# A long convolution by matrix transforms: even frequencies folded a second time, odd ones paired, 36 table blocks a round in place of 48

## The chip, the cores and the metric

The kernel runs on one core of a Trainium2 chip. The metric is the device time of one execution in microseconds, all of the network below included. An execution goes through two transformer-like blocks; the change touches one part of the first of them, the "Hyena" long convolution, and what stands just ahead of it and just behind it.

## The reference, cut to what matters

Two gated convolutions over the whole sequence (L = 1024 tokens, 512 channels). Each multiplies the spectrum of the signal by that of a two-sided filter of 2L taps. The filter is computed by a small network and weighted with a decay.

```python
def _hyena_filter_spectrum(L, w1, b1, fr1, w2, b2, fr2, w3):
    ...
    filt = filt * jnp.exp(-t * jnp.abs(deltas))[:, None, None, :]
    fwd = filt[:, :, 0]
    bwd = jnp.flip(filt[1:, :, 1], axis=0)
    two_sided = jnp.concatenate([fwd, zeros, bwd], axis=0)
    return jnp.fft.rfft(two_sided, axis=0)

def _hyena(hy, spec, skip):
    z, g1, g2 = u[..., :D_HYENA], u[..., D_HYENA:2 * D_HYENA], u[..., 2 * D_HYENA:]
    for o, gate in enumerate((g1, g2)):
        conv = jnp.fft.irfft(jnp.fft.rfft(z, n=2 * L, axis=1) * spec[:, o], n=2 * L, axis=1)[:, :L]
        z = gate * (conv + z * skip[o].astype(jnp.float32))
    return z
```

Ahead of it `hy = _short_conv_centred(proj[..., :HY_COLS], ...)` makes the signal and the gates (a matmul and three taps per channel), and behind it stands `_group_rms_norm(_hyena(hy, spec, hy_skip[l]), hy_norm_g[l], HYENA_GROUPS)`.

## The kernel before

Every fp32 operand is split in a rounded high part and a low part (`Split`), and a product of two of them is three matmuls (`mm3`, lines 193 to 195). The high part is made by ScalarE, the low part by VectorE or GpSimd, which subtract.

**The projection (`phase_conv_proj`, 230 to 428 us of the span).** Twelve tiles of 128 channels. For tile n TensorE does 96 matmuls in two halves; between the halves it makes filter taps (line 714), which need two psum banks that VectorE clears in `weigh` (lines 732, 733). Then ScalarE copies the tile out of psum (lines 892, 893), VectorE adds the two neighbouring taps (lines 932, 935), and TensorE turns the tile by eight transposes (line 848) one tile later. VectorE's program in a tile is: the two neighbour taps, `fold` of one filter tile (line 763; in the first tile of each filter four copies of one row, line 768), `weigh`. Tokens lie in the order 0 to 512, then 1023 down to 513, so that cosines and sines need one half of the sequence.

**The convolution (`phase_convolve`, 428 to 728 us).** Two rounds, one per gate. A round has three stages of 16 units; a unit is one table block of 4 x 128 x 128 numbers and, on TensorE, 12 matmuls of 128x512, apart from the `exact` rows and columns (lines 1011, 1012: two matmuls each).
- Filter stage (`filter_pe`): the filter's spectrum. It needs the four blocks of the folded filter (1 MB each, loaded, rounded by ScalarE in `fold_high`, line 1181, lowered by VectorE in `fold_low`, line 1252). ScalarE copies the result (lines 1210, 1211), which frees the banks (`act_free`).
- Signal stage (`signal_pe`): the signal's spectrum, two units for each of eight frequency tiles j. VectorE multiplies with the filter's spectrum (lines 1285 to 1288, `dve_done`), GpSimd adds the cross terms (lines 1241, 1242, `pool_done`), ScalarE rounds (lines 1188, 1189, `w_hi`), VectorE lowers (line 1258, `y_lo`).
- Inverse stage (lines 1147 to 1167): back to tokens. Tile j is read out by ScalarE and VectorE (lines 1227, 1298, 1299), multiplied with the gate (line 1308) and, in the second round, squared and summed (lines 1315, 1316), while TensorE goes on with tile j + 1.

The tables go through a ring of four buffers: SyncE loads block u when TensorE has finished unit u - 4 (line 983), ScalarE rounds it (`high`, line 988), GpSimd lowers it (`low`, line 993), and TensorE waits for that (`ft_lo`). What sets the order is the program of each engine as it is written: an engine that waits holds all that stands behind it. `until(u)` on ScalarE says how far it runs ahead with `high` before it waits for something else:

```python
            def until(u):
                while ahead[0] < min(u + 3, 2 * ROUND):
                    tables.high(act, ahead[0])
                    ahead[0] += 1
```

and GpSimd runs four table blocks ahead:

```python
                for j in range(TT):
                    for u in (B + UNITS + 2 * j + 4, B + UNITS + 2 * j + 5):
                        tables.low(pool, u)
                    pool.wait_ge(R.sem("dve_done"), R.at("dve_done", j + 1))
```

## Time and profile before

| | us |
|---|---|
| median of 3 runs (lowest, highest) | 3569.22 (3565.95, 3570.24) |
| the profiled execution | 3566.57 |
| its span, first to last instruction | 3564.8 |
| projection, convolution, group norm in it | 230 to 428, 428 to 728, 728 to 742 |
| TensorE, VectorE, ScalarE, GpSimd busy (share of the span) | 3332.7 (93%), 1758.4 (49%), 1112.2 (31%), 560.6 (16%) |
| mean granted TensorE clock | 0.971 |

The times of the rows are microseconds from the start of the span. Successive matmuls overlap in the records, so what one costs is the distance between two starts, not its duration.

### The profile page before, as it was taken

The numbers are of one execution on the slowest core, as the hardware profiler recorded it, in microseconds if no ns is written. First come the engines' busy times: TensorE is split into PE (matmuls) and PEld (weight loads), VectorE is DVE, ScalarE is ACT, GpSimd is POOL, SyncE is SP. The second block draws the span as 40 slices with busy tenths as digits, with TensorE's granted clock in tenths as the row PEclk, the third lists the DMA queues.
The fourth block names the chain that finished last, engine by engine and source line by source line (L and its number), as shares of the span: only waits on it lengthen the run. The fifth ranks groups of instructions, "written<-read, shape, count | busy, mean of one in ns | idle before, by whom it ended". The sixth has DMA issues, their size and how long they took to land. (4 is left out here: it accounts for less than half of the span.)

```text
span 3564.8 us, 40485 instructions
## 1 busy us (share of the span) xinstructions
PE 3332.7 (93%) x15544; PEld 2663.5 (75%) x15544; DVE 1758.4 (49%) x2739; ACT 1112.2 (31%) x2015; POOL 560.6 (16%) x378
## 2 busy tenths in 40 slices
PE   7999899976898899999999998988999899999998
PEld 5777688865786678888888776775567688888886
DVE  4415655565422446555544539789654332332434
ACT  4323344354322222111111433136674221211112
POOL 0002466722000001000001200000263200010010
PEclk9999999987999999999999999999999999999999
DMA  3232324412121113333321301123333121111111
GB/s 115 87 104 70 130 88 136 142 61 92 54 71 59 42 59 95 100 102 105 104 83 62 105 18 42 48 57 90 76 73 113 30 71 48 47 47 47 51 43 59
DMA packets 223644, 269.80 MB, mean 76 GB/s; under 512 B 17277, under 2 KB 150294, under 8 KB 221062
## 3 DMA queue, kind: packets, MB, share of 16 engines
q1 hardware_dynamic: 223496, 267.78, 24.4%
q8 instruction: 98, 1.61, 0.2%
q14 instruction: 50, 0.41, 0.0%
HBM read 219.16 MB, written 29.18 MB: 70 GB/s over the span
## 5 line engine op out<-in xcount | busy, mean ns | idle before, releaser
L193 PE MATMUL psum<-rounded,rounded 128*128 128x512 f32 (+2 forms) x3936 | 1537.7, 391 | 64.6 <-DVE rounded L222 51.6
L194 PE MATMUL psum<-rounded,rounded 128*128 128x512 f32 (+2 forms) x3936 | 1528.7, 388 | 0.0
L195 PE MATMUL psum<-rounded,rounded 128*128 128x512 f32 (+2 forms) x3936 | 1528.2, 388 | 0.0
L193 PEld LDWEIGHTS psum<-rounded,rounded 128*128 128x128 f32 x3936 | 746.6, 190 | 239.1 <-DVE rounded L222 56.8
L195 PEld LDWEIGHTS psum<-rounded,rounded 128*128 128x128 f32 x3936 | 746.1, 190 | 151.8
L194 PEld LDWEIGHTS psum<-rounded,rounded 128*128 128x128 f32 x3936 | 747.2, 190 | 148.9 <-issue 0.2
L3002 DVE TENSOR_TENSOR plain<-psum,plain 128x512 f32<-128x512 f32 x432 | 288.6, 688 | 110.4 <-PE psum L195 108.8
L3013 DVE TENSOR_TENSOR plain<-psum,plain 128x512 f32<-128x512 f32 x44 | 30.4, 692 | 425.1 <-ACT plain L2917 425.1
L3579 POOL TENSOR_TENSOR plain<-plain,plain 128x128 f32<-128x128 f32 (+3 forms) x64 | 97.3, 1530 | 563.4 <-ACT plain L3680 506.4
L3376 DVE TENSOR_SCALAR_CACHE_REDUCE plain<-plain,plain 128x384 bf16<-128x384 f32 (+2 forms) x204 | 181.8, 942 | 1.4
L2994 DVE TENSOR_TENSOR rounded<-plain,rounded 128x512 fp32r<-128x512 f32 x108 | 96.9, 897 | 166.0 <-ACT rounded L2906 165.9
L2917 ACT ACTIVATE plain<-psum 128x512 f32<-128x512 f32 x44 | 26.3, 598 | 454.6 <-PE psum L195 454.6
L2965 POOL TENSOR_TENSOR plain<-plain 128x512 f32<-128x512 f32 x64 | 67.0, 1047 | 597.2 <-ACT plain L2919 597.2
L993 POOL TENSOR_TENSOR rounded<-plain,rounded 128x512 fp32r<-128x512 f32 x96 | 143.6, 1505 | 101.2 <-ACT rounded L988 101.2
L2977 POOL TENSOR_TENSOR plain<-plain,plain 128x1024 f32<-128x1024 f32 x22 | 52.6, 2395 | 658.0 <-DMA plain<-in_w_down_dram 658.0
L2919 ACT ACTIVATE plain<-psum 128x512 f32<-128x512 f32 x64 | 38.3, 599 | 374.4 <-PE psum L195 374.4
L2941 ACT ACTIVATE rounded<-plain 128x1024 fp32r<-128x1024 f32 x54 | 57.0, 1056 | 278.4 <-DMA plain<-in_ff_w_dram 157.2
L3601 DVE CUSTOM_DVE_ANT_0 plain<-psum,plain 128x128 f32<-128x128 f32 (+7 forms) x128 | 96.2, 754 | 96.1 <-PE psum L3184 35.8
L3507 PE MATMUL psum<-plain,plain 128*128 128x128 f32 x576 | 86.9, 278 | 28.2 <-ACT plain L3664 26.8
L3653 ACT ACTIVATE plain<-plain,plain 128x128 f32<-128x128 f32 (+7 forms) x128 | 99.0, 773 | 37.5 <-DVE plain L3601 36.4
L988 ACT ACTIVATE rounded<-plain 128x512 fp32r<-128x512 f32 x96 | 60.5, 632 | 147.3 <-DMA plain<-in_c_fwd_dram 96.6
L2376 ACT ACTIVATE plain<-psum 128x1024 f32<-128x1024 f32 (+1 forms) x33 | 28.8, 872 | 237.1 <-PE psum L195 237.1
(326 smaller groups left out, 3457.5 us busy)
## 6 DMA issues: line engine op xcount, KB each, us to landing
plain<-in_ff_w_dram SPq DMA_DIRECT2D x64, 512.0 KB, 5.4
plain<-in_w_ada_dram SPq DMA_DIRECT2D x96, 256.0 KB, 3.5
plain<-in_w_gu_dram SPq DMA_DIRECT2D x44, 512.0 KB, 5.0
plain<-in_w_in_dram SPq DMA_DIRECT2D x36, 512.0 KB, 4.0
rounded<-rounded SPq DMA_DIRECT2D x72, 256.0 KB, 3.4
plain<-in_c_fwd_dram SPq DMA_DIRECT2D x64, 256.0 KB, 2.6
plain<-in_w_down_dram SPq DMA_DIRECT2D x22, 512.0 KB, 3.7
fold<-plain SPq DMA_DIRECT2D x8, 1024.0 KB, 4.8
```

Source lines behind the costliest of these rows:

```text
L193: nc.tensor.matmul(out, wh, xh, start=first, stop=False)
L194: nc.tensor.matmul(out, wh, xl, start=False, stop=False)
L195: return nc.tensor.matmul(out, wl, xh, start=False, stop=last)
L993: self.core.nc.gpsimd.tensor_tensor(w.lo, w.raw, w.hi_raw, ALU.subtract).then_inc(S["ft_lo"].sem, 1)
L2965: nc.gpsimd.tensor_tensor(full[half], first[half], first[half], ALU.mult).then_inc(S["square_done"].sem, 1)
L2994: nc.vector.tensor_tensor(ft[b].lo[:, f, cols], full[half], ft[b].hi_raw[:, f, cols], ALU.subtract).then_inc(S["ft_lo"].sem, 1)
L3002: nc.vector.tensor_tensor(hv, ps[:, 4 + t % 4, :], hv, ALU.add).then_inc(S["dve_free"].sem, 1)
L3376: self.after(nc.vector.tensor_scalar(self.flags[c % 2][:, 0:w], sel_tile(self.core, i), self.bound[:, c:c + 1], None, op, ALU.add, accum_o ...
L3507: last = nc.tensor.transpose(ps[:, 4 + j // 4, (j % 4) * P:(j % 4 + 1) * P], probs[n % 3][:, j * P:(j + 1) * P], core.ident)
L3579: nc.gpsimd.tensor_tensor(masked(n)[:, 0:w], slanted[h % 2][:, L - w:L], sel_tile(core, i), ALU.add).then_inc(S["pool_done"].sem, 1)
L3601: nc.vector.tensor_tensor_reduce(out=probs[n % 3][:, 0:w], in0=pair(n, w), in1=b, scale=-SCALE, scalar=3.0e38, op0=ALU.add, op1=ALU.min, a ...
L3653: nc.scalar.activation(probs[n % 3][:, 0:w], probs[n % 3][:, 0:w], ACT.Exp, scale=-1.0, bias=least[:, one], accum_out=total[:, one]).then_ ...
```

## The change

- Tokens lie in a new order (even and odd ones apart, `TOKENS`, `COLUMNS`), so that signal and inverse fold twice for even frequencies and in pairs for odd ones. The four tokens on the fold's edges are kept in four columns beside the tile (`t[:, L:L + 4]`).
- A round has 16 units in the filter stage as before, 12 in the signal stage and 8 in the inverse stage. In matmuls: filter 206 for 210, signal 166 for 210, inverse 114 for 210, which is 486 for 630 in a round.
- In the projection ScalarE has one more instruction per tile, VectorE three more small taps and a copy of four columns; `fold` copies a row in the second tile of each filter too.
- VectorE mends two pairs of rows of the loaded filter (`fix_folds`) before any `fold_low` but the first of round 1, and folds the signal in two steps of 1024 elements (`fold_signal`).
- GpSimd runs three table blocks ahead, and no block of the inverse stage is lowered ahead of the last cross terms. In the signal stage ScalarE runs fewer blocks ahead, and waits for the pairing (`paired`).
- The inverse stage's results stay in psum and in `kept_sums` until all of a parity are there; adding, gating and squaring come after the last of them.
- The group norm no longer mirrors (no `reverse`), and writes to strided columns.

```diff
 
                 ins.then_inc(S["fold_chain"].sem, 1)
-                dve.wait_ge(S["fold_chain"].sem, S["fold_chain"].at(4 * o + q + 1))
-                ins = nc.vector.tensor_copy(out[0:1, :], (a if q % 2 else b)[0:1, :])
+                dve.wait_ge(S["fold_chain"].sem, S["fold_chain"].at(8 * o + 4 * j + q + 1))
+                row = ((0, 0, 3, 2), (0, 2, 1, 3))[j][q]
+                ins = nc.vector.tensor_copy(out[0:1, :], self.both[0:1, row, :])
         ins.then_inc(S["pair_folded"].sem, 1)
 
     def close(self):
...
+                        last = nc.tensor.transpose(ps[:, 4 + t // 4, (t % 4) * P:(t % 4 + 1) * P], tmp[m % 2][:, TOKENS[t]], core.ident)
                     last.then_inc(S["tr_done"].sem, 1)
...
                 w1, bias = core.colsA[:, CW_HY + 12 + n:CW_HY + 13 + n], core.colsA[:, CB_HY + n:CB_HY + n + 1]
-                nc.scalar.activation(tmp[n % 2][:, 0:513], pr[:, 0:513], ACT.Identity, scale=w1, bias=bias)
-                nc.scalar.activation(tmp[n % 2][:, 513:L], pr[:, L - 1:512:-1], ACT.Identity, scale=w1, bias=bias).then_inc(S["act_done"].sem, 1)
+                t, pr2 = tmp[n % 2], quarters(pr)
+                nc.scalar.activation(quarters(t)[:, :, 1:256], pr2[:, :, 1:256], ACT.Identity, scale=w1, bias=bias)
+                nc.scalar.activation(quarters(t)[:, :, 257:512], pr2[:, :, 511:256:-1], ACT.Identity, scale=w1, bias=bias)
...
+                chain(last)
+                nc.vector.tensor_copy(t[:, 0:L].rearrange("p (b a c) -> p a b c", a=2, b=2)[:, :, :, 0], t[:, L:L + 4].rearrange("p (a b) -> p a b", a=2)).then_inc(S["dve_done"].sem, 1)
                 if 1 <= f <= NF:
                     filters.fold(dve, f - 1)
                 if 0 <= f < NF:
                     filters.weigh(dve, f, 0)
     for n in ("mm_done", "dve_done", "act_free", "tr_done", "act_done", "w_hi", "w_lo"):
         S[n].close(n_tiles)
-    S["dve_chain"].close(n_tiles)
+    S["dve_chain"].close(2 * n_tiles)
...
+            tables.products(pe, one, B + n, zfold, cos, True, j >= 2)
+            if j < 2:
+                exact(nc, one, mats[:, ALT_ROW, :], quarter, 0, last=True, rows=1)
+            ins = tables.products(pe, two, B + n, zfold, sin, True, j != 0, block=2)
+            if j == 0:
+                exact(nc, two, mats[:, ONE_COL, :], zfold, 0)
+                exact(nc, two, mats[:, NEG_COL, :], zfold, 1)
+                ins = exact(nc, two, mats[:, ONE_COL, :], quarter, 0, last=True, rows=1)
+            ins.then_inc(done, 1)
+        else:
+            u = B + 2 * n - 4
+            tables.products(pe, one, u, zfold, range(4, 8), True, True).then_inc(done, 1)
+            tables.products(pe, two, u + 1, zfold, range(0, 4), True, False)
+            mm3(nc, two, eighth[0:1, 0, :], eighth[0:1, 1, :], quarter.hi[0:1, 0, :], quarter.lo[0:1, 0, :], False, True).then_inc(done, 1)
...
+            n = 2 * p + part
+            one, two = ps[:, 2 * n, :], ps[:, 2 * n + 1, :]
+            src = Y_S if part else Y_R
+            pe.wait_ge(R.sem("dve_done"), R.at("dve_done", 5 + n))
+            pe.wait_ge(R.sem("y_lo"), R.at("y_lo", 4))
+            tables.products(pe, one, B + n, y, (src, src + 1), True, False)
+            ins = tables.products(pe, two, B + n, y, (src + 2, src + 3), True, False, block=2)
+            if part == 0:
+                ins = exact(nc, one, mats[:, NEG_ROW if p else ONE_ROW, :], y, Y_S, rows=1)
+            elif p == 0:
+                exact(nc, one, mats[:, ONE_COL, :], y, Y_R)
+                exact(nc, one, mats[:, ONE_COL, :], y, Y_R + 1)
+                ins = exact(nc, one, mats[:, ONE_COL, :], y, Y_S, rows=1)
...
+                        nc.scalar.activation(quarter.hi[0:1, 0, :], quarter.raw[0:1, 0, :], ACT.Copy).then_inc(R.sem("z_hi"), 1)
+                for n in range(4):
+                    until(B + signal_done(n))
+                    act.wait_ge(R.sem("pool_done"), R.at("pool_done", n + 1))
+                    nc.scalar.activation(y.hi[:, n::TT, :], y.raw[:, n::TT, :], ACT.Copy).then_inc(R.sem("w_hi"), 1)
+                for b in range(2):
+                    until(B + signal_done(5 + 2 * b))
+                    act.wait_ge(R.sem("paired"), R.at("paired", b + 1))
+                    nc.scalar.activation(y.hi[:, 4 + b:TT:2, :], y.raw[:, 4 + b:TT:2, :], ACT.Copy)
+                    nc.scalar.activation(y.hi[:, TT + 4 + b::2, :], y.raw[:, TT + 4 + b::2, :], ACT.Copy).then_inc(R.sem("w_hi"), 1)
+                until(B + INVERSE_AT + 4)
+                if R.o == 0:
...
-                        tables.low(pool, u)
-                    pool.wait_ge(R.sem("dve_done"), R.at("dve_done", j + 1))
+                low = B + SIGNAL_AT + 3
+                for n, j in enumerate(SIGNAL_ORDER):
+                    while low < min(B + signal_done(n) + 3, B + INVERSE_AT):
+                        tables.low(pool, low)
+                        low += 1
+                    pool.wait_ge(R.sem("dve_done"), R.at("dve_done", n + 1))
                     nc.gpsimd.tensor_tensor(yr[:, j, :], yr[:, j, :], cross[:, j, :], ALU.subtract)
-                    nc.gpsimd.tensor_tensor(ys[:, j, :], ys[:, j, :], cross[:, 8 + j, :], ALU.add).then_inc(R.sem("pool_done"), 1)
-                for u in range(B + 2 * UNITS + 4, B + ROUND):
...
+                if R.o == 0:
+                    fix_folds(R)
+                    for n in range(4):
+                        fold_low(R, n)
+                fold_signal(R)
                 if R.o == 1:
-                    dve.wait_ge(rounds[0].sem("tile_gated"), rounds[0].at("tile_gated", 4))
...
+                def pair(b):
+
+                    dve.wait_ge(R.sem("pool_done"), R.at("pool_done", 6 + 2 * b))
+                    one, two = y.raw[:, 4 + b::TT, :], y.raw[:, 6 + b::TT, :]
+                    chain(nc.vector.tensor_tensor(one, one, two, ALU.add))
+                    nc.vector.scalar_tensor_tensor(out=two, in0=two, scalar=-2.0, in1=one, op0=ALU.mult, op1=ALU.add).then_inc(R.sem("paired"), 1)
+
...
+                            last = nc.vector.tensor_tensor(terms[:, p, 3, :], other, own, ALU.subtract)
+                    last.then_inc(R.sem("dve_free"), 1)
+                if R.o == 0:
+                    fix_folds(rounds[1])
+                    fold_low(rounds[1], 1)
...
+                dve.wait_ge(R.sem("dve_free"), R.at("dve_free", 2))
+                for p in range(2):
+                    near, far = hy[:, 2 * p:2 * p + 2, 0:DH], hy[:, 4 + 2 * p:6 + 2 * p, 0:DH]
+                    nc.vector.tensor_tensor(near, terms[:, p, 0:2, :], terms[:, p, 2:4, :], ALU.add)
+                    chain(nc.vector.tensor_tensor(far, terms[:, p, 0:2, :], terms[:, p, 2:4, :], ALU.subtract))
...
+                        chain(nc.vector.tensor_tensor(hy[0:1, 4, 0:DH], u, rows[1], ALU.subtract))
+                    for n, (made, t) in enumerate(((near, 2 * p), (far, 4 + 2 * p))):
+                        nc.vector.tensor_tensor(made, made, gates[:, t:t + 2, :], ALU.mult).then_inc(R.sem("tile_gated"), 1)
+                        if R.o == 1:
+                            dve.wait_ge(R.sem("tile_gated"), R.at("tile_gated", 2 * p + n + 1))
+                            chain(nc.vector.tensor_tensor(squares, made, made, ALU.mult))
```

What stands on the engines in a row, at three places. In these listings `rounded_512` are the table blocks, `rounded_8192` and `plain_8192` the product y or the filter's blocks, `plain_12288` the signal and the gates.

GpSimd, before, from the cross terms of the seventh frequency tile of a signal stage on:

```order
L1241 TENSOR_TENSOR plain_8192_57<-plain_8192_57,plain_8192_58 128x512 [waits dve_done]
L1242 TENSOR_TENSOR plain_8192_57<-plain_8192_57,plain_8192_58 128x512
L993 TENSOR_TENSOR rounded_512_1502<-plain_512_1503,rounded_512_1501 128x512 [waits ft_hi]
L993 TENSOR_TENSOR rounded_512_1506<-plain_512_1507,rounded_512_1505 128x512 [waits ft_hi]
L1241 TENSOR_TENSOR plain_8192_57<-plain_8192_57,plain_8192_58 128x512 [waits dve_done]
L1242 TENSOR_TENSOR plain_8192_57<-plain_8192_57,plain_8192_58 128x512
L993 TENSOR_TENSOR rounded_512_1494<-plain_512_1495,rounded_512_1493 128x512 [waits ft_hi]
L993 TENSOR_TENSOR rounded_512_1498<-plain_512_1499,rounded_512_1497 128x512 [waits ft_hi]
```

and GpSimd now, from the same tile on:

```order
L1364 TENSOR_TENSOR plain_8192_57<-plain_8192_57,plain_8192_58 128x512 [waits dve_done]
L1365 TENSOR_TENSOR plain_8192_57<-plain_8192_57,plain_8192_58 128x512
L1364 TENSOR_TENSOR plain_8192_57<-plain_8192_57,plain_8192_58 128x512 [waits dve_done]
L1365 TENSOR_TENSOR plain_8192_57<-plain_8192_57,plain_8192_58 128x512
L1071 TENSOR_TENSOR rounded_512_1494<-plain_512_1495,rounded_512_1493 128x512 [waits ft_hi]
L1071 TENSOR_TENSOR rounded_512_1498<-plain_512_1499,rounded_512_1497 128x512 [waits ft_hi]
L1071 TENSOR_TENSOR rounded_512_1502<-plain_512_1503,rounded_512_1501 128x512 [waits ft_hi]
```

Before, four blocks of the inverse stage are lowered ahead of the last cross terms (lines 1241, 1242) or with them; now the first block of the inverse stage comes behind the last cross terms (lines 1364, 1365).

ScalarE, before, in a signal stage, from the first rounding of y on:

```order
L1188 ACTIVATE rounded_8192_55<-plain_8192_57 128x512 [waits pool_done]
L1189 ACTIVATE rounded_8192_55<-plain_8192_57 128x512
L988 ACTIVATE rounded_512_1493<-plain_512_1495 128x512 [waits table0]
L988 ACTIVATE rounded_512_1497<-plain_512_1499 128x512 [waits table1]
L1188 ACTIVATE rounded_8192_55<-plain_8192_57 128x512 [waits pool_done]
L1189 ACTIVATE rounded_8192_55<-plain_8192_57 128x512
L988 ACTIVATE rounded_512_1501<-plain_512_1503 128x512 [waits table2]
L988 ACTIVATE rounded_512_1505<-plain_512_1507 128x512 [waits table3]
L1188 ACTIVATE rounded_8192_55<-plain_8192_57 128x512 [waits pool_done]
L1189 ACTIVATE rounded_8192_55<-plain_8192_57 128x512
```

and ScalarE now:

```order
L1333 ACTIVATE rounded_8192_55<-plain_8192_57 128x2x512 [waits pool_done]
L1066 ACTIVATE rounded_512_1493<-plain_512_1495 128x512 [waits table0]
L1333 ACTIVATE rounded_8192_55<-plain_8192_57 128x2x512 [waits pool_done]
L1066 ACTIVATE rounded_512_1497<-plain_512_1499 128x512 [waits table1]
L1333 ACTIVATE rounded_8192_55<-plain_8192_57 128x2x512 [waits pool_done]
L1066 ACTIVATE rounded_512_1501<-plain_512_1503 128x512 [waits table2]
L1333 ACTIVATE rounded_8192_55<-plain_8192_57 128x2x512 [waits pool_done]
L1066 ACTIVATE rounded_512_1505<-plain_512_1507 128x512 [waits table3]
L1066 ACTIVATE rounded_512_1493<-plain_512_1495 128x512 [waits table0]
L1066 ACTIVATE rounded_512_1497<-plain_512_1499 128x512 [waits table1]
```

Before there are two table blocks between two roundings of y; now one, for the first four, and then four blocks.

VectorE, before, from the end of the first round's inverse stage to the signal's fold of the second:

```order
L1308 TENSOR_TENSOR plain_12288_1492<-plain_2048_2891,plain_12288_1492 128x512 [waits dve_free]
L1308 TENSOR_TENSOR plain_12288_1492<-plain_2048_2891,plain_12288_1492 128x512
L1252 TENSOR_TENSOR rounded_8192_56<-plain_8192_54,rounded_8192_55 128x2048 [waits fold_hi] x2
L1268 TENSOR_TENSOR plain_4096_2886<-plain_12288_1492 128x512 [waits tile_gated]
L1271 COPY plain_4096_2886<-plain_12288_1492 1x512 [waits dve_chain]
L1268 TENSOR_TENSOR plain_4096_2886<-plain_12288_1492 128x512 x4
L1271 COPY plain_4096_2886<-plain_12288_1492 1x512 [waits dve_chain]
L1268 TENSOR_TENSOR plain_4096_2886<-plain_12288_1492 128x512 x3
```

and VectorE now, from the repaired rows of the second round's filter to its last `fold_low` (of the gating and of `fold_signal`, 20 instructions, those left out by the two pieces are of the same kinds):

```order
L1388 SCALAR_TENSOR_TENSOR plain_8192_54<-plain_8192_54 1x512 [waits dve_chain]
L1388 SCALAR_TENSOR_TENSOR plain_8192_54<-plain_8192_54 1x512
L1375 TENSOR_TENSOR rounded_8192_56<-plain_8192_54,rounded_8192_55 128x2048 [waits fold_hi]
L1479 TENSOR_TENSOR plain_12288_1492<-plain_4096_2986 128x2x512 [waits dve_free]
L1480 TENSOR_TENSOR plain_12288_1492<-plain_4096_2986 128x2x512
L1483 TENSOR_TENSOR plain_12288_1492<-plain_2048_2985,plain_512_2984 1x512 [waits dve_chain]
L1484 TENSOR_TENSOR plain_12288_1492<-plain_2048_2985,plain_512_2984 1x512
```

```order
L1401 TENSOR_TENSOR plain_4096_2976<-plain_4096_2977 128x1024 [waits dve_chain]
L1402 TENSOR_TENSOR plain_4096_2976<-plain_4096_2977 128x1024
L1401 TENSOR_TENSOR plain_4096_2976<-plain_4096_2977 128x1024
L1402 TENSOR_TENSOR plain_4096_2976<-plain_4096_2977 128x1024
L1405 TENSOR_TENSOR plain_4096_2976<-plain_12288_1492 1x512 [waits dve_chain]
L1406 COPY plain_4096_2976<-plain_12288_1492 1x512
L1408 TENSOR_TENSOR plain_512_2980<-plain_12288_1492 1x512
L1375 TENSOR_TENSOR rounded_8192_56<-plain_8192_54,rounded_8192_55 128x2048 [waits fold_hi] x2
```

Before, the two last `fold_low` (line 1252, x2) stand ahead of the signal's fold; now they stand behind all of the gating (lines 1479 to 1488) and of the fold (lines 1395 to 1408).

## Rows read from the trace of the kernel before

**Rows 1.** The page, part 1: busy us, share of the span, instructions.
```profile
PE 3332.7 (93%) x15544; PEld 2663.5 (75%) x15544; DVE 1758.4 (49%) x2739; ACT 1112.2 (31%) x2015; POOL 560.6 (16%) x378
```

**Rows 2.** Waits of TensorE, 433.5 to 722: total, times, longest.
```profile
PE psum L193 <- DVE rounded L1252: 6.8, 1, 6.8
```

**Rows 3.** Stretches: length, then busy us and count of each engine, clock.
```profile
core 0: us, PE busy (x) PEld busy (x) DVE busy (x) ACT busy (x) POOL busy (x), PEclk, DMA share, GB/s
433.00:438.00 5.00, 4.54 (x11) 3.57 (x12) 4.45 (x3) 4.07 (x3) 4.83 (x2) 0.50 1.00 371
500.00:560.00 60.00, 60.00 (x265) 49.48 (x264) 37.62 (x41) 21.35 (x37) 49.87 (x35) 1.00 0.48 158
```

**Rows 4.** Groups of 433.5 to 722: count, busy us, mean ns, idle before.
```profile
L193 PE MATMUL psum<-rounded,rounded 128*128 128x512 f32 x384 | 150.6, 392 | 6.8 <-DVE rounded L1252 6.8
L1012 PE MATMUL psum<-rounded,rounded 128*128 128x512 f32 x54 | 21.0, 389 | 0.0
L1241 POOL TENSOR_TENSOR plain<-plain,plain 128x512 f32<-128x512 f32 x16 | 27.0, 1684 | 0.0
L988 ACT ACTIVATE rounded<-plain 128x512 fp32r<-128x512 f32 x93 | 58.8, 632 | 146.4 <-DMA plain<-in_c_fwd_dram 96.6 <-DMA plain<-in_c_inv_dram 49.8
```

**Rows 5.** Timeline of VectorE and ScalarE at the first round's start: start, duration.
```profile
431.11 2.29 DVE L1252 TENSOR_TENSOR rounded<-plain,rounded 128x2048 fp32r<-128x2048 f32 x1 [4.02 <-ACT rounded L1181]
436.76 1.91 ACT L1181 ACTIVATE rounded<-plain 128x2048 fp32r<-128x2048 f32 x1 [0.88 <-DMA plain<-fold]
```

**Rows 6.** Timeline of TensorE at the first round's start.
```profile
433.46 0.80 PE L193 MATMUL psum<-rounded,rounded 128*128 128x512 f32 x1 [6.75 <-DVE rounded L1252]
```

**Rows 7.** Timeline of the projection, VectorE and TensorE.
```profile
311.16 0.42 DVE L768 COPY plain<-plain 1x512 f32<-1x512 f32 x1
314.93 1.55 PE L714 MATMUL psum<-plain,plain 64*128 64x512 f32 x3 [1.36 <-DVE plain L733]
395.52 0.68 DVE L733 TENSOR_TENSOR plain<-psum,plain 128x512 f32<-128x512 f32 x1
396.63 1.98 PE L714 MATMUL psum<-plain,plain 64*128 64x512 f32 x4
404.12 1.03 PE L848 MATMUL psum<-plain,plain 128*128 128x128 f32 x8
```

**Rows 8.** Timeline of VectorE: an instruction of 4 columns, in another stage.
```profile
766.34 0.16 DVE L2081 SCALAR_TENSOR_TENSOR plain<-psum,plain 128x4 f32<-128x4 f32 x1 [1.92 <-PE psum L1926]
```

**Rows 9.** Timeline of the signal stage, GpSimd, VectorE, ScalarE.
```profile
496.38 1.29 POOL L1241 TENSOR_TENSOR plain<-plain,plain 128x512 f32<-128x512 f32 x1
498.88 1.29 POOL L993 TENSOR_TENSOR rounded<-plain,rounded 128x512 fp32r<-128x512 f32 x1
499.61 0.68 DVE L1288 TENSOR_TENSOR plain<-psum,plain 128x512 f32<-128x512 f32 x1
502.17 2.55 DVE L1258 TENSOR_TENSOR rounded<-plain,rounded 128x512 fp32r<-128x512 f32 x2 [1.88 <-ACT rounded L1189]
502.43 1.74 POOL L1241 TENSOR_TENSOR plain<-plain,plain 128x512 f32<-128x512 f32 x1
504.64 0.68 DVE L1285 TENSOR_TENSOR plain<-psum,plain 128x512 f32<-128x512 f32 x1
```

**Rows 10.** Timeline of ScalarE: one pass over 1024 elements.
```profile
389.61 1.02 ACT L863 ACTIVATE plain<-psum 128x1024 f32<-128x1024 f32 x1
```

**Rows 11.** Timeline of VectorE at the second round's start.
```profile
581.91 5.58 DVE L1252 TENSOR_TENSOR rounded<-plain,rounded 128x2048 fp32r<-128x2048 f32 x2
589.23 1.40 DVE L1271 COPY plain<-plain 1x512 f32<-1x512 f32 x1
```

**Rows 12.** Timeline of the convolution's end, TensorE, ScalarE and VectorE.
```profile
719.11 0.60 ACT L1227 ACTIVATE plain<-psum 128x512 f32<-128x512 f32 x1 [4.46 <-PE psum L195]
721.40 0.39 PE L195 MATMUL psum<-rounded,rounded 128*128 128x512 f32 x1
725.73 1.23 DVE L1315 TENSOR_TENSOR plain<-plain 128x1024 f32<-128x1024 f32 x1
726.99 1.22 DVE L1316 TENSOR_REDUCE plain<-plain 128x16 f32<-128x1024 f32 x1
730.39 0.55 DVE L1355 RECIPROCAL plain<-plain 128x64 f32<-128x64 f32 x1 [2.18 <-ACT plain L1375]
```

540 lines of the change are left out of this document (309 added, 231 removed).

## The prediction

> **What bounds the kernel now.** I read the page's busy line first: TensorE is busy for 3332.7 us of the span, 93%, and no other engine reaches half [rows 1]. So the convolution's time is the number of its matmuls times their pitch, as long as TensorE waits for nothing there. The waits of that stretch say so: one wait, 6.8 us, at its start [rows 2]; the grouped lines give the same 6.8 for all 384 matmuls of a line and 0.0 for the exact rows [rows 4]. A stretch of 60 us in the middle gives the pitch: 60.00 busy, 265 matmuls, clock 1.00, so 0.2265 us each [rows 3]. It also warns: GpSimd is busy for 49.87 of these 60 us. It is the engine with the least room, and every table block goes through it. Behind the one wait 11 matmuls take 4.54 us at a granted clock of 0.50 [rows 3], 0.41 each: a long wait of TensorE costs some 2 us more than itself. Both together: 1260 x 0.2265 = 285.4, plus 12 x 0.19, is 287.7; the stretch took 721.8 - 433.5 = 288.3 [rows 6, 12].
>
> **A. Matmuls removed.** 630 - 486 is 144 in a round, 288 in both. 288 x 0.2265 = **-65.2 us**, if TensorE stays as busy as now. Sixty of the new matmuls contract over one row; I count them like the others, and no row shows one. The Trainium skill ("TensorE: Matmul & The Clock Gate", Why this matters for your kernels) says a matmul with small K takes the time of a full one; that agrees with the count. Were they free instead, 60 x 0.2265 = 13.6 us more would go; that is in the lower end.
>
> **B. Projection.** A tile's chain is psum full, ScalarE's copy, the neighbour taps, `fold`, `weigh`, TensorE's line 714. In an ordinary tile `weigh` ends at 395.52 + 0.68 = 396.20 and TensorE starts at 396.63: 0.43 us of room; in a filter's first tile it waits 1.36 already [rows 7]. The chain gets one more small instruction on ScalarE and four of four columns or fewer on VectorE. An instruction of 4 columns took 0.16 [rows 8]; with their order among themselves I take 0.75 a tile. Two first tiles +0.75 each; two second tiles also get four row copies at 0.42 [rows 7], +1.8 + 0.75 - 0.43 = 2.1 each; three others and the last +0.3 to 0.75; clock +1. **+8.5**, bounds 3 and 13. The transposes read tokens with a stride; eight take 1.03 [rows 7]. I cost that at nothing; if each took twice as long, the 96 would add 12.4.
>
> **C. First round's start.** `fold_low` (2.29, from 431.11) led straight to the first matmul at 433.46 [rows 5, 6]. Now `fix_folds` stands ahead of it on VectorE and waits for the fourth filter block, which lands just ahead of ScalarE's 436.76 [rows 5]. Then four row operations at about 0.6 (between the copy's 0.42 and the 1.40 of one of them beside GpSimd [rows 7, 11]) and `fold_low`: 436.76 + 2.4 + 2.3 = 441.5, which is **+8.0**, bounds 6 and 10.
>
> **D. Signal stage, twice.** Before, ScalarE has two table blocks between two roundings of y; now one, for the first four. So `high` of unit 20 waits for the GpSimd sums of the first tile, and so on for units 21 to 23, while GpSimd's next `low` waits for that `high`. One turn is: two cross terms, 2 x 1.29 alone or 2 x 1.74 beside VectorE's lowering (1.69 on average); rounding of 1024 elements 1.02; `high` 0.63; `low` 1.29 [rows 4, 9, 10]. That is 5.5 to 6.4 us, for a unit that TensorE eats in 12 x 0.2265 = 2.7 (3.4 with its exact ones). Four turns cost about 4 x 2.8, less the two blocks in store, some 6 to 8. Then unit 27 stands behind the first pairing (products 0.68 each, sums 2 x 1.3, pair 2 x 1.3, rounding 2.0, `high`, `low`), some 6 more. With 2 of clock the stage lasts about 54 against 166 x 0.2265 = 37.6: **+16.5** each, **+33**, bounds 10 and 21 each.
>
> What the rows show of the two engines: the same cross term takes 1.29 us while VectorE reads psum and 1.74 while it subtracts two SBUF operands [rows 9]. The Trainium skill ("GPSIMD Engine Reference", 1. Specifications) says that GpSimd shares its SBUF interfaces with VectorE and collides with instructions of two SBUF inputs; the trace agrees. The pairing is such an instruction, 1024 elements long. By the rule the sums beside it take 3.5 a pair, without it 2.6: 0.9 a turn, within my bounds.
>
> **E. Inverse stage's start, twice.** The first inverse block is lowered behind the last cross terms; before, four were ahead. TensorE ends the signal stage; then VectorE's products 2.6 (four at 0.68), the sums 2.6 to 3.5, `low` 1.3: 6.5 to 7.4 us, of which I take 7.4 since the pairing runs beside them, and 2 of clock. **+18.8** for both, bounds 12 and 24.
>
> **F. Middle of the second round's filter stage.** From the last matmul of round 0 (T) VectorE does the last terms (to T + 2.1), `fix_folds` (4.7), `fold_low` behind ScalarE's 1.91 [rows 5] (9.2), the gating, 8 x 1.2 and 4 x 0.6 (21), `fold_signal`, 8 x 1.2 and three row operations (33), and the last two `fold_low`, 5.58 [rows 11], to 38 or, with GpSimd beside it, 41. (1.2 is the 1.23 of 1024 elements [rows 12].) ScalarE waits for them ahead of its first copies and of the next `high`; copies, `high`, `low` take 3.1: unit 8 of the stage starts at T + 41 to 44. TensorE is there at 8 x 12.9 x 0.2265 = 23.3, and 2.3 for stall and clock on the way, T + 25.6. That is 17 on average, 2 of clock, and 1 for small stalls on the way: **+20**, bounds 14 and 24. Before, `fold_low` stood ahead of the fold and no wait was there [rows 2].
>
> **G. The tail.** Before, the last tile is read out and gated and the squares are summed from the last matmul, 721.8, to 728.2 [rows 12], 6.4 us. Now nothing of a parity's work starts before all of it is there: terms 2.1, sums and differences 2.4, rows 2.4, four times gate 1.2, square 1.23, reduction 1.22 [rows 12], and 2.4 for the other parity's sums: 24.0. **+17.6**, bounds 15 and 20.
>
> The group norm loses its mirror, and writes with a stride: nothing, it is outside the chain by a row at 730.39 with a wait of 2.18 [rows 12].
>
> **Sum.** -65.2 + 8.5 + 8.0 + 33 + 18.8 + 20 + 17.6 = +40.7. On the profiled execution's 3566.6 that is 3607.3; the median stands 2.65 above that execution, so **3610**. All lower ends, the free one-row matmuls left out: -65.2 + 3 + 6 + 20 + 12 + 14 + 15 = +4.8; all upper: -65.2 + 13 + 10 + 42 + 24 + 24 + 20 = +67.8, and 80 with the slow transposes.
>
> **Rivals.**
> 1. *The waits are covered (faster).* If ScalarE and GpSimd run far enough ahead for D, E and F to close to nothing, B at 2, C and G stay: -65.2 + 2 + 8.0 + 17.6 = -37.6, 3532. For it: TensorE waits nowhere there now [rows 2]. Against it: the order of instructions itself puts `low` of the first inverse block behind the last cross terms, and these behind TensorE's last signal matmul; no duration makes that 0. Faster by over 7 us needs D, E and F together under 24 (65.2 - 8.5 - 8.0 - 17.6 - 7), where I have 72. 12%.
> 2. *The signal stage is looser.* TensorE's own waits push the products later, so the turns don't add up: D 5 each, F 14. -65.2 + 8.5 + 8.0 + 10 + 18.8 + 14 + 17.6 = +11.7, 3581. For it: 4 buffers in the ring. Against it: GpSimd 83% busy [rows 3]. 12%.
> 3. *More.* Transposes with a stride at twice the time (+12.4), and half clock for twice as long after each wait (some +12: the six waits of D, E and F at 2 each): +65, 3634. For it: the clock of 0.50 behind a wait of 6.75 [rows 3, 6]; against it: no row of a strided transpose. 12%.
> 4. *It cancels,* within 7 us of before, which is 0.2% and about what a measurement can tell from none: one sum among many between 1 and 2. 6%.
>
> My own forecast holds 58%, by itself 3588 to 3632. Range **3576 to 3640**: it leaves out the first and the last case and the tail of the third; its low end is the sum of all lower ends, 3574, nearly. Faster by over 0.2%: 0.13 (the first rival and a sliver of the second); same 0.06; slower 0.81.
>
> **What would show it.** In the changed kernel's profile: 972 matmuls in the convolution; waits of TensorE on GpSimd's `low` (line 1071) of units 20 to 23 and 27, and one of about 7 us at unit 28, in each round; one of over 15 us in the middle of the second filter stage, with VectorE's line 1375 behind it; 24 us from the last matmul to VectorE's last reduction (line 1492); the first convolution matmul 8 us later relative to the projection's end; and half clock behind each. From the projection's end to the last reduction it should be 32 us longer than now (the sum without B: 40.7 - 8.5). It is wrong if the waits of D, E and F together are below 50 us, or if a row shows the strided transposes or the four-column operations at more than twice what I took.

## The result, and the profile after

The changed kernel takes 3637.73 us (median of 4 runs, 3633.0 to 3641.34) against 3567.59 for the kernel before (median of 4, 3564.54 to 3570.24): ratio 1.0196, 95% interval 1.0178 to 1.0214. That is 70 us slower, where 41 were forecast; it lies in the range of 3576 to 3640. Its profiled execution took 3641.34, with a span of 3639.5 us: it is the longest of the four, 3.6 us above the median.

The busy line of the page first:

```profile
PE 3300.7 (91%) x15240; PEld 2618.2 (72%) x15240; DVE 1785.0 (49%) x2794; ACT 1098.2 (30%) x1982; POOL 532.1 (15%) x354
```

TensorE has 304 instructions less than in [rows 1] (288 of them convolution matmuls), yet its busy time fell by 32.0 us only, where 288 x 0.2265 are 65.2. The rest is matmuls that ran slower. Where it waits, from the first matmul of the convolution on:

```profile
PE psum L253 <- POOL rounded L1071: 63.5, 14, 17.7
PE psum L253 <- DVE rounded L1375: 15.0, 1, 15.0
```

The one wait of [rows 2], 6.8 us, is now 15.0 and ends at the first matmul; behind it are fourteen new ones, 63.5 us, all for GpSimd's `low` (line 1071). The stages (filter, signal, inverse of the first round, then of the second), all cut 0.2 us behind the start of their first matmul:

```profile
457.29:509.18 51.89, 50.36 (x207) 40.09 (x208) 30.54 (x21) 24.56 (x34) 32.94 (x15) 0.95 0.27 76
509.18:577.15 67.97, 47.32 (x167) 33.63 (x166) 31.77 (x41) 14.48 (x21) 38.17 (x28) 0.86 0.23 66
577.15:606.51 29.36, 29.36 (x115) 22.59 (x116) 12.50 (x11) 10.64 (x16) 13.59 (x9) 0.92 0.49 170
606.51:677.67 71.16, 50.57 (x207) 39.43 (x206) 46.69 (x39) 27.79 (x38) 28.32 (x16) 0.88 0.21 59
677.67:744.48 66.81, 46.00 (x167) 32.61 (x166) 31.82 (x41) 14.37 (x21) 38.21 (x28) 0.88 0.23 67
744.48:773.97 29.49, 29.27 (x114) 22.19 (x114) 10.22 (x10) 7.85 (x13) 11.04 (x7) 0.93 0.44 161
```

The columns are those of [rows 3]; a window counts the matmul at its border twice. At 0.2265 us a matmul the stages would take 46.7, 37.6 and 25.8. Two things stand out: the signal stage lasts 67 to 68 us though GpSimd is busy for 38 of them only (no engine is full, they wait for each other), and the granted clock is below 1 in every stage. The waits themselves, on TensorE's timeline (start of the matmul behind the wait, idle time in brackets):

```profile
457.08 0.79 PE L253 MATMUL psum<-rounded,rounded 128*128 128x512 f32 x1 [15.05 <-DVE rounded L1375]
529.03 0.50 PE L253 MATMUL psum<-rounded,rounded 128*128 128x512 f32 x1 [2.80 <-POOL rounded L1071]
540.96 0.80 PE L253 MATMUL psum<-rounded,rounded 128*128 128x512 f32 x1 [2.88 <-POOL rounded L1071]
561.81 0.79 PE L253 MATMUL psum<-rounded,rounded 128*128 128x512 f32 x1 [5.98 <-POOL rounded L1071]
576.93 0.76 PE L253 MATMUL psum<-rounded,rounded 128*128 128x512 f32 x1 [8.41 <-POOL rounded L1071]
652.62 0.76 PE L253 MATMUL psum<-rounded,rounded 128*128 128x512 f32 x1 [17.67 <-POOL rounded L1071]
801.62 1.11 PE L1563 MATMUL psum<-plain,plain 128*128 128x128 f32 x4 [27.87 <-DVE plain L1537]
```

In order: `fix_folds` (C), two turns of the signal stage (units 21 and 23 of the round) and its last block (unit 27; all three D), the first inverse block (unit 28, E), the middle of the second filter stage (unit 8, F), the tail (G). Unit 22 waits for 0.6 us, unit 20 not at all. The second round repeats these waits of D and E to 0.1 us. The lock-step of the signal stage, one turn on ScalarE and GpSimd:

```profile
525.53 1.06 ACT L1333 ACTIVATE rounded<-plain 128x1024 fp32r<-128x1024 f32 x1 [4.43 <-POOL plain L1365]
526.50 0.61 ACT L1066 ACTIVATE rounded<-plain 128x512 fp32r<-128x512 f32 x1
527.19 1.79 POOL L1071 TENSOR_TENSOR rounded<-plain,rounded 128x512 fp32r<-128x512 f32 x1 [1.69 <-ACT rounded L1066]
528.94 1.29 POOL L1364 TENSOR_TENSOR plain<-plain,plain 128x512 f32<-128x512 f32 x1
530.19 1.27 POOL L1365 TENSOR_TENSOR plain<-plain,plain 128x512 f32<-128x512 f32 x1
533.15 1.79 POOL L1071 TENSOR_TENSOR rounded<-plain,rounded 128x512 fp32r<-128x512 f32 x1 [1.69 <-ACT rounded L1066]
```

From one `low` to the next 5.96 us: low 1.8, two sums 2.5, rounding of y 1.0, rounding of the block 0.6. Each engine waits for the other in turn.

In the projection the waits for `weigh` are these; before there were 2, of 1.36 us each, the first in [rows 7]:

```profile
PE psum L780 <- DVE plain L799: 9.6, 7, 2.3
```

The matmuls over one row had no row in the trace before. Here are three, between two of 128 rows:

```profile
545.03 0.39 PE L255 MATMUL psum<-rounded,rounded 128*128 128x512 f32 x1
545.35 0.49 PE L253 MATMUL psum<-rounded,rounded 1*128 1x512 f32 x1
545.68 0.39 PE L254 MATMUL psum<-rounded,rounded 1*128 1x512 f32 x1
545.92 0.39 PE L255 MATMUL psum<-rounded,rounded 1*128 1x512 f32 x1
546.24 0.51 PE L253 MATMUL psum<-rounded,rounded 128*128 128x512 f32 x1
546.58 0.40 PE L254 MATMUL psum<-rounded,rounded 128*128 128x512 f32 x1
```

Their starts are 0.32, 0.33, 0.24, 0.32 and 0.34 us apart, where 0.23 is the pitch: a group costs some 0.4 us more than three full matmuls.

And the end, VectorE behind the last matmul (which ends at 773.75):

```profile
774.42 0.69 DVE L1466 TENSOR_TENSOR plain<-plain,psum 128x512 f32<-128x512 f32 x1 [1.43 <-ACT plain L1350]
796.89 1.22 DVE L1492 TENSOR_REDUCE plain<-plain 128x16 f32<-128x1024 f32 x1
```

24.4 us from the last matmul's end to the last reduction's, against 6.4 in [rows 12].

### The profile page after: what moved, and what is told of

Same layout as the page of the kernel before. It is cut to its first block and busy times, and to the rows that moved or that the text cites. A ratio compares the mean times of both kernels' runs of the same rounds, so it can differ in the third digit from the quotient of the medians.

```text
span 3639.5 us, 39821 instructions
## 1 busy us (share of the span) xinstructions
PE 3300.7 (91%) x15240; PEld 2618.2 (72%) x15240; DVE 1785.0 (49%) x2794; ACT 1098.2 (30%) x1982; POOL 532.1 (15%) x354
## 5 line engine op out<-in xcount | busy, mean ns | idle before, releaser
L253 PE MATMUL psum<-rounded,rounded 128*128 128x512 f32 (+2 forms) x3848 | 1517.2, 394 | 138.3 <-POOL rounded L1071 63.5
L254 PE MATMUL psum<-rounded,rounded 128*128 128x512 f32 (+2 forms) x3848 | 1502.9, 391 | 0.0
L255 PE MATMUL psum<-rounded,rounded 128*128 128x512 f32 (+2 forms) x3848 | 1501.8, 390 | 0.0
L253 PEld LDWEIGHTS psum<-rounded,rounded 128*128 128x128 f32 x3848 | 735.8, 191 | 327.9 <-DVE rounded L282 57.1
L255 PEld LDWEIGHTS psum<-rounded,rounded 128*128 128x128 f32 x3848 | 735.1, 191 | 150.5
L254 PEld LDWEIGHTS psum<-rounded,rounded 128*128 128x128 f32 x3848 | 736.5, 191 | 146.0 <-issue 0.2
L3751 POOL TENSOR_TENSOR plain<-plain,plain 128x128 f32<-128x128 f32 (+3 forms) x64 | 97.3, 1530 | 565.5 <-ACT plain L3852 507.3
L3166 DVE TENSOR_TENSOR rounded<-plain,rounded 128x512 fp32r<-128x512 f32 x108 | 97.3, 901 | 164.8 <-ACT rounded L3078 164.7
L3089 ACT ACTIVATE plain<-psum 128x512 f32<-128x512 f32 x44 | 26.3, 598 | 455.4 <-PE psum L255 455.4
L1071 POOL TENSOR_TENSOR rounded<-plain,rounded 128x512 fp32r<-128x512 f32 x72 | 122.4, 1710 | 146.0 <-ACT rounded L1066 145.9
L3698 PE MATMUL psum<-plain,plain 128*64 128x256 f32 (+1 forms) x704 | 99.1, 365 | 0.8 <-ACT plain L3836 0.8
```

The source lines that it names most:

```text
L253: nc.tensor.matmul(out, wh, xh, start=first, stop=False)
L254: nc.tensor.matmul(out, wh, xl, start=False, stop=False)
L255: return nc.tensor.matmul(out, wl, xh, start=False, stop=last)
L1071: self.core.nc.gpsimd.tensor_tensor(w.lo, w.raw, w.hi_raw, ALU.subtract).then_inc(S["ft_lo"].sem, 1)
L3166: nc.vector.tensor_tensor(ft[b].lo[:, f, cols], full[half], ft[b].hi_raw[:, f, cols], ALU.subtract).then_inc(S["ft_lo"].sem, 1)
L3698: last = nc.tensor.matmul(out, va[:, j, column:column + HD], tiled(turned[b][:, j, :])[:, seen, :], start=j == 0, stop=j == 4 * b + tiles[1])
```

## The experiments

The parent of each is the changed kernel (3637.7 us) unless said otherwise; the ratios are to the kernel before, run beside it. The changed kernel's own interval is 1.0178 to 1.0214. Those of a3, a4, b2, b3 and b4 overlap it, so their differences of 4.9 to 11.2 us are rough, and the stages in the traces carry the reading.

**a1_low: inverse blocks lowered ahead of the last cross terms.**

```diff
-                    while low < min(B + signal_done(n) + 3, B + INVERSE_AT):
+                    while low < B + signal_done(n) + 3:
```

> The changed kernel, but GpSimd may lower blocks of the inverse stage ahead of the last cross terms. Theory (the order on GpSimd makes the wait of 8.4 us at the first inverse block, in each round): both waits of 8.4 us go, with some 3 us of half clock behind each; but the fifth inverse block needs the second pairing lowered, which comes 14 to 16 us after the end of the signal stage where four inverse blocks take 11.7, so a new wait of 2 to 4.5 us stands there. In all -14 us against the changed kernel's 3637.7 (between -10 and -20). Rival (GpSimd has too much work in the stage and is late whatever its order): the wait stays within 2 us, and the time within 4 us of 3637.7.

Measured 3622.48, ratio 1.0153 (1.0136 to 1.0170): -15.2. The wait of 8.4 is gone, and a new one stands behind three inverse blocks, since `low` runs three blocks ahead and the fourth is again behind the last cross terms (a block earlier than expected):

```profile
577.60 0.47 PE L253 MATMUL psum<-rounded,rounded 128*128 128x512 f32 x1 [2.50 <-POOL rounded L1071]
```

The theory of E holds.

**a2_high: ScalarE one block more ahead in the signal stage.**

```diff
-                    until(B + signal_done(n))
+                    until(B + signal_done(n) + 1)
...
-                    until(B + signal_done(5 + 2 * b))
+                    until(B + signal_done(5 + 2 * b) + 1)
```

> The changed kernel, but ScalarE rounds one table block more before it waits in the signal stage. Theory (lock-step of 6.0 us a turn, of which the rounding of y 1.0 and of the block 0.6 go): a turn is 4.3 us, the waits of 2.8 and 2.9 us go, and so does the one of 6.0 us before the stage's last block, with half clock behind them; the wait of 8.4 us at the first inverse block stays. 2 x (5.7 + 6.0 + 2 to 3) = -28 us against 3637.7 (between -20 and -32). Rival (GpSimd's own work, 28 instructions of 1.3 to 1.8 us in the stage, is the bound): at most -6 us.

Measured 3605.90, ratio 1.0105 (1.0088 to 1.0122): -31.8, as much as the upper end. A turn is now 4.7 us, of its waits 0.6 and 1.7 us are left (for 2.8, 0.6 and 2.9), the 6.0 us before the stage's last block are gone, and the 8.4 stay. The row is the first round's signal stage, 68.0 us before:

```profile
505.68:557.21 51.53, 40.90 (x167) 29.91 (x166) 32.84 (x41) 15.35 (x22) 41.67 (x28) 0.94 0.29 87
```

GpSimd has the same 28 instructions and was not the bound.

**d2_lowhigh: both edits.**

> The changed kernel with only the two edits of the first runs together (GpSimd lowers inverse blocks early; ScalarE one block more ahead in the signal stage). Theory (the two waits are apart from each other): -15.2 - 31.8 = -47, 3591 (between 3586 and 3596), and the signal stage with what follows loses the 8.4 us in both rounds. Rival (with ScalarE ahead GpSimd is the bound, and the lower blocks taken early push its cross terms back): at least 6 us less than the sum, 3597 or more.

Measured 3600.25, ratio 1.0090 (1.0074 to 1.0105): -37.5, and so 9.5 us less than the sum. The rival's size is right, its reason is not shown: `high` of the first inverse block now stands behind the first pairing's rounding on ScalarE, and a wait is left there.

```profile
547.42 1.04 ACT L1338 ACTIVATE rounded<-plain 128x1024 fp32r<-128x1024 f32 x1
548.37 1.65 ACT L1066 ACTIVATE rounded<-plain 128x512 fp32r<-128x512 f32 x3
549.06 1.27 POOL L1071 TENSOR_TENSOR rounded<-plain,rounded 128x512 fp32r<-128x512 f32 x1 [7.14 <-ACT rounded L1066]
550.48 0.77 PE L253 MATMUL psum<-rounded,rounded 128*128 128x512 f32 x1 [2.47 <-POOL rounded L1071]
```

GpSimd waits 7.1 us for ScalarE ahead of it: it has time. Two edits that each end at the next wait do not add.

**a3_fold: the second round's filter blocks early.** On ScalarE their `fold_high` moves likewise, to behind that of the second block, with `until(B + 1)` ahead of it.

```diff
                 fold_signal(R)
-                if R.o == 1:
-                    fold_low(R, 2)
-                    fold_low(R, 3)
...
                     fix_folds(rounds[1])
-                    fold_low(rounds[1], 1)
+                    for n in range(1, 4):
+                        fold_low(rounds[1], n)
```

> The changed kernel, but in the second round ScalarE rounds and VectorE lowers the last two filter blocks right behind the second, ahead of the gating and of the signal's fold, and ScalarE rounds one table block ahead of them. Theory (the wait of 17.7 us in the middle of the filter stage is VectorE's order): it goes, with 3 to 4 us of half clock, and the wait of 2.4 us with it; the fold of the signal ends when it ends now, a little late for the signal stage, 1 to 2 us. In all -20 us against 3637.7 (between -15 and -24). Rival (VectorE's work of 43 us in the stage is the bound, in any order): the wait comes back at the start of the signal stage, and the gain is under 8 us.

Measured 3631.69, ratio 1.0179 (1.0162 to 1.0196), -6.0: the theory fails. The wait of 17.7 became one of 10.6 further on. ScalarE, which had waited for `fold_low`, now waits for the signal's fold, with the same table blocks behind it:

```profile
641.12 1.91 ACT L1323 ACTIVATE rounded<-plain 128x2048 fp32r<-128x2048 f32 x1 [13.42 <-DVE plain L1399]
```

**b2_fold: the same, and the signal's rounding late in the second round.**

```diff
-                    if 1 <= j <= 2:
+                    q = j - 4 * R.o
+                    if 1 <= q <= 2:
```

> The changed kernel with the filter blocks of the second round lowered early, as in the run before, and with ScalarE's rounding of the folded signal moved in that round from the tiles 1 to 3 to the tiles 5 and 6, so that no table block stands behind it while VectorE still folds. Theory (the wait moved from one instruction of ScalarE to another, and both hold the blocks behind them): the 10.6 us that came back go too, and the 2.9 before them stay; VectorE's fold ends 44 us after the round's start, the signal stage needs it at 47 and behind a rounding and a lowering of 1.9 + 2.3 us, so 2 to 4 us are left at the stage's start. -19 us against the changed kernel's 3637.7 (between -14 and -23). Rival (VectorE's work is the bound in any order): the wait comes back whole at the signal stage's start, -6 us as in the run before.

Measured 3629.41, ratio 1.0169 (1.0152 to 1.0186), -8.3: nearer to the rival's -6 than to the theory's -19. The filter stage falls from 71.2 to 62.0 us; the wait is now 8.6 at its end, for VectorE's last lowering of the signal, and more of the next stage runs at half clock (0.78 for 0.88):

```profile
599.38:661.36 61.98, 49.88 (x206) 39.15 (x205) 58.12 (x39) 29.93 (x41) 33.98 (x18) 0.92 0.25 72
661.36:733.90 72.54, 51.85 (x168) 36.45 (x167) 32.17 (x41) 12.06 (x17) 35.95 (x26) 0.78 0.19 58
```

VectorE is busy for 58.1 of 62.0 us there, so it is what bounds the stage, and that is 11.4 us more than in the changed kernel's row of it (46.69), with the same 39 records. What stretches it is in its timeline:

```profile
635.17 1.21 DVE L1394 TENSOR_TENSOR plain<-plain 128x1024 f32<-128x1024 f32 x1
636.30 2.31 DVE L1393 TENSOR_TENSOR plain<-plain 128x1024 f32<-128x1024 f32 x1
```

The same kind of instruction takes 1.21 us, or 2.31 where GpSimd lowers a block beside it. (The Trainium skill, "GPSIMD Engine Reference", 1. Specifications, has the two share their SBUF interfaces; the trace agrees, and shows that both pay.)

**a4_rows: full matmuls in place of those over one row.** `rows=1` is left out of all `exact` calls, and three calls read another operand besides (two of them are shown). The count and the order of the matmuls stay; what the added rows contribute is not what the reference computes.

```diff
-                exact(nc, one, mats[:, ALT_ROW, :], quarter, 0, last=True, rows=1)
+                exact(nc, one, mats[:, ALT_ROW, :], zfold, 0, last=True)
...
-            mm3(nc, two, eighth[0:1, 0, :], eighth[0:1, 1, :], quarter.hi[0:1, 0, :], quarter.lo[0:1, 0, :], False, True)
+            mm3(nc, two, mats[:, ONE_COL, :], mats[:, NEG_COL, :], zfold.hi[:, 0, :], zfold.lo[:, 0, :], False, True)
```

> The changed kernel, but its 60 matmuls over one row run over all 128 rows of a tile that is there (other numbers, the same count and order; what the rows add to the result is changed where it was one row of a tile of one row). Theory of the prediction (a matmul over one row takes the time of a full one): no change, within 3 us of 3637.7. Theory from the trace after (the distances between starts go from 0.23 to 0.32 and 0.34 us at each change from 128 rows to one and back, some 0.4 us for each of 26 groups): -11 us (between -8 and -13). A third, that one-row matmuls save time: slower by 5 us or more.

Measured 3630.60, ratio 1.0173 (1.0156 to 1.0190): -7.1, less than the 11 expected but not 0. The first round's filter stage went from 51.9 us, its length in every execution that has it unchanged, to 51.0. The second round's signal and inverse stages, ten of the groups, last 96.3 to 96.6 us together in the changed kernel, a3, b3, b4 and b5, and 93.3 here. (The first round's can't be read: unchanged, they last 93.8 to 97.3.) A matmul over one row is neither free nor the same: the change of the number of rows costs. (The Trainium skill, "TensorE: Matmul & The Clock Gate", Why this matters for your kernels, gives a single matmul over 32 rows the time of a full one. For one over one row beside its like, 0.24 us, the trace agrees; at the change it does not.)

**b3_start: the first filter block ahead of `fix_folds`.**

```diff
                     fold_high(R, 0)
-                    until(0)
+                    until(1)
...
+                    fold_low(R, 0)
                     fix_folds(R)
-                    for n in range(4):
+                    for n in range(1, 4):
                         fold_low(R, n)
```

> The changed kernel, but in the first round VectorE lowers the first filter block ahead of fix_folds, and ScalarE rounds the fourth table block ahead of the second filter block. Theory (the 8.3 us more of wait at the convolution's start are fix_folds, which waits for the fourth filter block): the first matmul comes 8 us earlier; its first four units take 10.9 us, and the second filter block is lowered 1 to 2 us too late for the fifth, with the fifth table block behind it. -6 us against 3637.7 (between -3 and -9). Rival (the wait is the load's, which nothing on VectorE shortens): the wait only moves to the fifth unit, within 2 us.

Measured 3632.83, ratio 1.0176 (1.0159 to 1.0193): -4.9. The wait is 6.73, that of [rows 6] again. The filter stage grew from 51.9 to 55.8: its wait of 1.5 us at unit 3 went, and waits of 1.0, 0.3 and 2.8 us came at units 4, 9 and 10.

**b4_small: without the four columns beside the tile.** The small taps of VectorE are left out of its two lists likewise, and ScalarE's two other instructions start a column earlier. What the fold's edges need is not computed.

```diff
-                nc.scalar.activation(t[:, L:L + 4], pr[:, 0:L:256], ACT.Identity, scale=w1, bias=bias).then_inc(S["act_done"].sem, 1)
...
-                chain(last)
-                nc.vector.tensor_copy(t[:, 0:L].rearrange("p (b a c) -> p a b c", a=2, b=2)[:, :, :, 0], t[:, L:L + 4].rearrange("p (a b) -> p a b", a=2)).then_inc(S["dve_done"].sem, 1)
+                last.then_inc(S["dve_done"].sem, 1)
```

> The changed kernel, but in the projection the four columns kept beside the tile are left out: ScalarE's third instruction of a tile, VectorE's three small taps and its copy (what they hold is then taken from the neighbouring order, so the tokens at the fold's edges are wrong); the row copies of the second tiles stay. Theory (the chain of a tile got 0.6 to 0.75 us longer by them): the seven waits of TensorE for weigh, 9.6 us in all, fall to about 5, and some of the half clock behind them goes: -7 us against 3637.7 (between -4 and -9). Rival (row copies and strides make it): within 2 us.

Measured 3626.56, ratio 1.0165 (1.0148 to 1.0182): -11.2, more than expected.

```profile
PE psum L780 <- DVE plain L799: 5.1, 4, 1.3
```

Seven waits of 9.6 us became four of 5.1. From the projection's first matmul to the convolution's it takes 210.5 us, for 219.0 in the changed kernel's trace and 215.9 to 219.4 in the six kernels that left this part alone (a1, a2, a3, a4, b2, d2).

**b5_weigh: `weigh` ahead of `fold`.**

```diff
-                if 1 <= f <= NF:
-                    filters.fold(dve, f - 1)
                 if 0 <= f < NF:
                     filters.weigh(dve, f, 0)
+                if 1 <= f <= NF:
+                    filters.fold(dve, f - 1)
```

> The changed kernel, but VectorE does weigh ahead of fold in each tile of the projection. Theory (TensorE waits for weigh alone, and fold with its row copies stands ahead of it): all seven waits for weigh, 9.6 us, go and with them some 6 us of half clock: -15 us against 3637.7 (between -11 and -17), which is more than the change added to the projection. Rival (the copy out of psum and the taps are the chain, whatever stands behind): at most -4 us.

Measured 3624.56, ratio 1.0155 (1.0138 to 1.0172): -13.2. No wait for `weigh` is left. From the projection's first matmul to the convolution's it takes 203.5 us; without C, 7.7 here, that is 195.9, for 197.2 before: of B nothing is left.

**c1_all and c2_all: all orders mended.** a1, a2, b2, b3 and b5 together; `quarter` cleared to zero over 128 rows, so that 11 of 13 groups run over full rows whose other rows add nothing; the gating of the first parity ahead of the second's last terms. c2_all has besides:

```diff
+            for n, t in enumerate((0, 4, 2, 6)):
+                act.wait_ge(rounds[1].sem("tile_gated"), rounds[1].at("tile_gated", n + 1))
+                nc.scalar.activation(y.before[:, 2 * n:2 * n + 2, :], hy[:, t:t + 2, 0:DH], ACT.Square).then_inc(core.sig["gated_squared"].sem, 1)
```

> The changed kernel with all orders mended together: GpSimd lowers inverse blocks early, ScalarE rounds one block more ahead in the signal stage, the second round's filter blocks are lowered early with the signal's rounding late, the first filter block is lowered ahead of fix_folds, weigh stands ahead of fold; new here: the matmuls over one row run over 128 rows of which the others are zero (11 of 13 groups of a round), and the gating of one parity stands ahead of the other parity's last terms, in both rounds. Theory (the parts measured alone add up: -15.2, -31.8, -8.3, -4.9, -13.2 and 11/13 of -7.1; the earlier gating takes 2.5 us off the tail and some 4 off VectorE's work at the second round's start): -86, 3552 (between 3540 and 3562), faster than the kernel before at 3568. Rival (VectorE at the second round's start bounds the stage, and what is won before it is waited for there): 3565 to 3580.

> The same, with the squares of the last gating on ScalarE (VectorE reduces them behind its last gating). Theory (VectorE's 24 us of work behind the last matmul are the tail): four squares of 1.23 us leave VectorE, one of about 1.1 us stays in the chain: 3.5 us less than the run beside it, the tail from the last matmul to TensorE's next falls from 27.9 in the changed kernel to about 22. Rival (ScalarE loads a table for the square, and that is in the chain): within 1.5 us of the run beside it.

c1_all: 3566.40, ratio 0.9991 (0.9982 to 1.0000), -71.3 where the theory had -86. That is the rival's number, but only a small part of it is the rival's reason. Of the missing 14.7 us d2_lowhigh has 9.5, by a1 and a2 alone, with nothing changed at the second round's start. There the filter stage lasts 60.8 us for the some 58 expected (62.0 in b2_fold, less 4): the early gating brought a wait of 4.6 us for `dve_free`. The first filter stage is 1.3 longer than in b3_start, and the tail 1.5 shorter where 2.5 were expected. c2_all: 3562.84, ratio 0.9981 (0.9972 to 0.9990), 3.6 less, as expected, though by the traces the tail fell by more, from 26.3 to 19.9 us; no table was loaded for the square.

**d1_all: c2_all with the second round's start in a new order.**

```diff
-                    if p == 0:
+                    if p == 0 and R.o == 1:
                         gating(R, 0)
+                    if p == 0 and R.o == 0:
+                        fix_folds(rounds[1])
```

Behind each `fold_high(R, n)`, n below 3, stands `until(B + 1 + n)`; the first round's gating of both parities stands behind the filter blocks, and its folded signal is rounded from the fourth tile on.

> The last combined kernel (3562.8) with the second round's start ordered anew: fix_folds between the two parities' terms, where VectorE waits for ScalarE; the gating of both parities behind the filter blocks again (early gating in the last round alone); ScalarE rounds a table block behind each filter block, and the folded signal from the fourth tile on in the first round too. Theory (VectorE's chain from the end of round 0 to the signal's lowering, 60 us there, is the bound of that filter stage, and loses the 2.6 us of fix_folds, the 2 us of waiting for ScalarE and the 4.5 us that TensorE waited for the terms): that stage falls from 60.5 to about 56 us, the first round's loses its 2.8 us wait; -7 us, 3556 (between 3550 and 3560). Rival (what VectorE saves there it loses to GpSimd, whose table blocks then fall on more of its instructions of two inputs): 3561 to 3566.

3559.00, ratio 0.9971 (0.9962 to 0.9981), the fastest kernel here: 0.3% faster than the one before. -3.8 for c2_all, half of what was expected. The first round's filter stage fell by 6.2 us, from 54.8 to 48.6, and waits nowhere behind its first matmul; the second's only from 60.5 to 59.3. That is 7.4 us, of which the medians show half: in the two profiled executions the rest of the program, behind the tail, differs by 4.1 us the other way.

```profile
565.52:625.98 60.46, 51.03 (x207) 40.48 (x206) 54.52 (x41) 29.45 (x40) 32.50 (x17) 0.94 0.26 74
```

```profile
556.94:616.21 59.27, 47.51 (x207) 38.29 (x206) 55.59 (x39) 30.34 (x41) 37.60 (x18) 0.94 0.26 76
615.88 0.79 PE L253 MATMUL psum<-rounded,rounded 128*128 128x512 f32 x1 [8.63 <-DVE rounded L1449]
```

The first row is c2_all's, the others d1_all's. VectorE has fewer records and yet 1.1 us more busy time, GpSimd 5.1 more: in this stage it is as the rival says. The signal and inverse stages of d1_all, both rounds, show where more is left:

```profile
481.08:525.40 44.32, 38.61 (x167) 30.77 (x166) 27.17 (x39) 14.90 (x22) 32.61 (x24) 1.00 0.27 77
525.40:556.60 31.20, 28.51 (x114) 22.33 (x115) 18.09 (x15) 10.45 (x15) 20.53 (x13) 0.95 0.54 194
615.88:662.16 46.28, 40.61 (x166) 32.20 (x167) 27.16 (x39) 12.68 (x18) 30.01 (x22) 0.96 0.25 69
662.16:695.14 32.98, 28.69 (x114) 22.11 (x114) 15.64 (x13) 7.29 (x12) 17.01 (x11) 0.95 0.48 175
```

Together they last 154.8 us, where 560 matmuls at 0.2265 are 126.8. Of the 28 us between, 18.4 are waits, at units 22, 23, 28, 29 and 32 of each round; no run here takes them away.

## Why the prediction was right, and where its sizes were off

| step | forecast | measured | from |
|---|---|---|---|
| A, 288 matmuls | -65.2 | -65.2 | counts; 972 in the trace |
| B, projection | +8.5 | +13.5 | convolution's start, less C and 1.8 ahead of the projection |
| C, first start | +8.0 | +8.3 | 15.05 - 6.75 |
| first filter stage | 0 | +2.8 | excess over 46.7, less that of before |
| D and E, both rounds | +51.8 | +66.3 | 33.7 and 32.6, excess of signal and inverse stages, less that of before |
| F, second filter stage | +20 | +24.5 | 71.16 - 46.66 |
| G, tail | +17.6 | +17.9 | 27.87 - 9.94 |
| sum | +40.7 | +68.1 | |

The spans differ by 74.7 us; 1.8 of the rest stand ahead of the projection and 4.9 behind the group norm's first matmul. This last part varies from run to run: in the traces of all these kernels, whose code there is the same in work, it is 2833.0 to 2842.2 us long. It isn't explained by the change, and the medians differ by 70.1. The measured column is of one execution. Where other kernels left a part alone, it varies in theirs: B from 10.3 to 13.0 (six kernels), C from 7.9 to 9.1 (the same), the first round's D and E from 30.1 to 32.3 (a3, b2, b3, b4, b5). So B and the first round stand at their upper ends here.

**Right for the wrong sum.** By itself my forecast was to lie within 3588 to 3632; 3637.7 is outside, and in the range only because I had left room for the third rival, 3634. Half of this rival came true: half clock took some 18 us in D, E and F together where I had 10. Its other half didn't: the transposes over a stride cost 0.8 us, not 12.4. What made up for that had no place in any sum: the matmuls over one row, the first filter stage, and the 4.9 us behind the group norm. So the mechanism was forecast, and that the number fell inside the range is in part luck.

**Right:** that no wait could be covered by a duration, since the order makes them. C (8.3 for 8.0), G (24.4 for 24.0 us of VectorE behind the last matmul) and the turn of 6.0 us (for 5.5 to 6.4) came out to a few per cent. The first inverse block's wait was 8.4 for 6.5 to 7.4, unit 27's 6.0 for 6, the filter stage's 17.7 for 17. That the named orders are the causes a1 shows for E, a2 for D and b3 for C; for G c2 shows that the tail shrinks with VectorE's work. Of the signs named, the 972 matmuls are there, waits at units 21 to 23, 27 and 28 of each round but none at 20, and the waits of D, E and F are 62.0 us together, above 50. From the projection's end to the last reduction it is 54.6 us longer, though, not 32.

**Mis-sized: D and E.** I took 2 us of clock behind each stage's waits and nothing for rows. The first round's 33.9 us (33.7 and the 0.2 of before) can be taken apart by the distances between starts. Five waits are 20.7 us. 37 matmuls start 0.38 us or more behind the one before with no wait between, at half clock: 8.5 us, and 0.8 more at the five starts behind waits. The groups over one row are 3.5 us, 0.35 each for ten, and 0.4 is left. In the second round they are 20.8, 6.8 and 0.8, and 3.5 to 4. I had some 22 us of waits a round (14.5 in D, 7.4 in E), 4 of clock and 0 of rows. So the waits were sized right, the half clock at half of what it was, and the rows, put at nothing because no row showed one, were 7 us.

**Mis-sized: F.** 20.5 us are waits (2.5, 17.7 and 0.4), 2.7 half clock; of the 20 forecast 18 were waits and stalls and 2 clock. The rest is the change of rows and small steps.

**Mis-sized: B.** The waits for `weigh` grew by 6.8 us (9.6 for 2.7) and the one ahead of the last transposes by 0.7 (4.29 for 3.55), near the sum of the steps; I had put 1 us on the clock. TensorE's timeline shows what it was:

```profile
409.06 1.98 PE L780 MATMUL psum<-plain,plain 64*128 64x512 f32 x4 [2.11 <-DVE plain L799]
410.98 0.80 PE L253 MATMUL psum<-rounded,rounded 128*128 128x512 f32 x1
411.57 0.63 PE L254 MATMUL psum<-rounded,rounded 128*128 128x512 f32 x1
412.00 0.63 PE L255 MATMUL psum<-rounded,rounded 128*128 128x512 f32 x1
```

Starts 0.43 us apart behind a wait of 2.11, the pace at the granted clock of 0.50 in [rows 3]. The waits of before were 1.36 us long [rows 7], and none of these stretches stood behind them. Of 13.5 us 7.6 are waits and 0.8 the transposes (13.3 us for 96 by their starts, 12.5 before); the other 5.1 are matmuls that ran slower, for the most part this. Such a stretch does not follow from the wait's length alone: behind the first wait of the seven, 2.1 us in each trace, none stands in the changed kernel, a1, a2 and a4, and eight matmuls at half clock in a3, b2 and d2; b4 has five behind a wait of 1.28 us. Strided transposes cost next to nothing, as taken.

**Wrong in its reason: what a mended order would give.** F was sized by VectorE's row of work, and that was right; but I took the wait for `fold_low` to be its price. a3 and b2 show that the wait only moves: VectorE's work in that stage, busy for 46.7 us and up to 58.1 beside GpSimd, bounds it in any order tried. Nor is that stage the greater part of what is missing. Of the 65.2 us of matmuls removed, the best order found gives back 9.5. By its trace the convolution and tail of d1_all are 15.8 us shorter than before. Of the 49 us that are missing there, some 28 stand in the signal and inverse stages, 12.6 in the second filter stage (59.3 for 46.7), and 9.9 in the tail.

## What to carry to other kernels

Removing matmuls shortens a stage only as far as the engines that feed it have room, and these need not be full: GpSimd was busy for 38 of 68 us when TensorE waited for it. When work of a stage shrinks, ask for each block who prepares it, what stands ahead of that instruction, and on whom that waits. One table block more or less of running ahead was worth 32 us of 3638, half of what the removed matmuls were worth. Two such mends need not add: a1 and a2 together gave 9.5 us less than their sum. A wait of TensorE is to be priced with the half clock behind it: in the first round's signal and inverse stages 20.7 us of waits came with 9.3 us of it. And before a difference of a few microseconds is read from two traces, look at how long the same stage lasts in runs that left it alone.

## What the runs showed of the hardware

- A change between matmuls over 128 rows and over one row costs about 0.1 us at each of four starts (0.32, 0.33, 0.32 and 0.34 us where the pitch is 0.23), by the medians 7.1 us for 26 groups (a4_rows).
- VectorE and GpSimd slow each other: 1.21 to 2.31 us for VectorE's 1024 elements with two inputs, and for GpSimd four blocks in 9.0 us, where one alone takes 1.29 (changed kernel, second filter stage):

```profile
614.07 9.00 POOL L1071 TENSOR_TENSOR rounded<-plain,rounded 128x512 fp32r<-128x512 f32 x4 [5.57 <-ACT rounded L1066]
615.72 2.28 DVE L1479 TENSOR_TENSOR plain<-plain 128x1024 f32<-128x1024 f32 x1
```

- One-row instructions of VectorE suffer too: in the second round line 1484 took 1.77 us beside GpSimd's lowering, and 0.67 in the tail, with GpSimd idle.
- The same wait of 2.1 us in the same code was followed by none or by eight matmuls at half clock, most of them 0.43 us apart, from one trace to the next (none in the changed kernel's, a1, a2 and a4; eight in a3, b2 and d2).
